# Sixteen gate products between the last two matmuls of a weight chunk instead of behind them

## The reference, cut to what matters

```python
q = (xi @ w_query) ...                       # queries, scores against sub_keys
top_s, top_c = lax.top_k(cand, PEER_TOPK)    # 16 experts per token and head
g = jax.nn.softmax(top_s, axis=-1)
u = jnp.take(expert_down, idx, axis=0)
act = jax.nn.gelu(jnp.einsum('btd,bthkd->bthk', xi, u))
v_sel = jnp.take(expert_up, idx, axis=0)
return jnp.einsum('bthk,bthkd->btd', g * act, v_sel)
```

## Time and profile before

| what | us |
|---|---|
| median of 3 executions | 2059.5 (2059.19 to 2060.71) |
| the profiled execution, whole | 2064.05 |
| its span, from first to last instruction | 2062.2 |
| PE busy, of the span | 2041.3 (99%) |
| DVE busy | 1639.3 (79%) |
| ACT busy | 1356.3 (66%) |

### The profile page before, as it was taken

One profiled execution on the slowest core, in us unless ns is written; L12 is line 12 of the kernel. 1 busy time (PEld: TensorE's weight loads), 2 busy tenths in 40 slices (PEclk: granted clock), 3 DMA queues, 4 the chain that ended last, 5 costly groups with the idle time before them and its releaser, 6 DMA issues.

```text
span 2062.2 us, 31647 instructions
## 1 busy us (share of the span) xinstructions
PE 2041.3 (99%) x11776; PEld 1749.0 (85%) x11776; DVE 1639.3 (79%) x2971; ACT 1356.3 (66%) x2303; POOL 373.5 (18%) x183
## 2 busy tenths in 40 slices
PE   8999999999999999999999999999999999999998
PEld 7788988888888888887888888888888888888888
DVE  7968988889869999877589888899689998743456
ACT  6665688878756666566646888777566666544674
POOL 1448800000000000012378100000000000045341
PEclk9999999999999999999999999999999999999999
DMA  6455855555566566664357655555656555676444
GB/s 231 153 156 168 238 171 169 173 165 167 171 190 203 190 213 202 206 210 143 120 167 222 192 169 168 170 174 167 191 179 208 205 194 188 225 217 197 130 157 139
DMA packets 108461, 376.26 MB, mean 182 GB/s; under 512 B 12372, under 2 KB 17908, under 8 KB 107412
## 3 DMA queue, kind: packets, MB, share of 16 engines
q1 hardware_dynamic: 107444, 369.00, 56.8%
q0 software_dynamic: 864, 5.24, 1.2%
HBM read 367.87 MB, written 1.08 MB: 179 GB/s over the span
## 4 chain that ended last, share of the span: by engine, by line
PE 92%; DVE 5%; ACT 1%; DMA 1%; issue 1%; POOL 0%; SPq 0%; DVEq 0%; ACTq 0%
PE ps L211 29%; PE ps L212 14%; PE ps L205 14%; PE ps L207 14%; PE ps L206 14%; PE ps L1126 3%; DVE WL L192 1%; DMA raw<-in_l_up_dram 1%; PE ps L1105 1%; DVE arena L818 1%; PE ps L1149 1%; DVE arena L815 0%; PE ps L2394 0%; PE ps L2418 0%; PE ps L1152 0%
## 5 line engine op out<-in xcount | busy, mean ns | idle before, releaser
L186 ACT ACTIVATE WH<-raw 128x1024 fp32r<-128x1024 f32 (+1 forms) x680 | 701.7, 1036 | 304.5 <-PE ps L207 186.7
L211 PE MATMUL ps<-X,WH 128*128 128x512 f32 x2528 | 895.9, 398 | 0.1
L212 PE MATMUL ps<-X,WL 128*128 128x256 f32 x2528 | 707.0, 280 | 0.0
L192 DVE TENSOR_TENSOR WL<-raw,WH 128x1024 fp32r<-128x1024 f32 (+1 forms) x554 | 661.9, 1197 | 39.0 <-ACT WH L186 38.2
L198 POOL TENSOR_TENSOR WL<-raw,WH 128x1024 fp32r<-128x1024 f32 x126 | 319.1, 2556 | 1572.6 <-ACT WH L186 1570.5
L211 PEld LDWEIGHTS ps<-X,WH 128*128 128x128 f32 x2528 | 474.0, 188 | 107.8 <-issue 0.6
L212 PEld LDWEIGHTS ps<-X,WL 128*128 128x128 f32 x2528 | 477.2, 189 | 0.1
L205 PE MATMUL ps<-WH,X 128*128 128x512 f32 (+1 forms) x784 | 310.4, 396 | 1.6 <-DVE X L417 0.9
L207 PE MATMUL ps<-WH,X 128*128 128x512 f32 (+1 forms) x784 | 305.4, 390 | 0.0
L206 PE MATMUL ps<-WL,X 128*128 128x512 f32 (+1 forms) x784 | 305.1, 389 | 0.0
L205 PEld LDWEIGHTS ps<-WH,X 128*128 128x128 f32 x784 | 147.5, 188 | 36.9 <-issue 4.5
(11 more groups left out here) (355 smaller groups left out, 2640.2 us busy)
## 6 DMA issues: line engine op xcount, KB each, us to landing
raw<-in_l_down_dram SPq DMA_DIRECT2D x256, 512.0 KB, 3.6
raw<-in_l_up_dram SPq DMA_DIRECT2D x256, 512.0 KB, 4.2
raw<-in_l_wq_dram SPq DMA_DIRECT2D x32, 512.0 KB, 3.5
raw<-in_w_qk_dram SPq DMA_DIRECT2D x24, 512.0 KB, 3.7
raw<-in_w_gates_dram SPq DMA_DIRECT2D x24, 512.0 KB, 3.5
raw<-in_l_nat_dram SPq DMA_DIRECT2D x16, 512.0 KB, 3.5
raw<-in_l_wout_dram SPq DMA_DIRECT2D x16, 512.0 KB, 3.6
raw<-in_l_win_dram SPq DMA_DIRECT2D x16, 512.0 KB, 4.0
```

The lines of the kernel that those rows point to most:

```text
L186: a.activation(WH[:, i % NW, 0:w], raw[:, i % NW, 0:w], ACT.Copy).then_inc(w_high, 1)
L192: v.tensor_tensor(WL[:, i % NW, 0:w], raw[:, i % NW, 0:w], WH[:, i % NW, 0:w], ALU.subtract).then_inc(w_low_v, 1)
L211: t.matmul(PS[:, bank, :], w[0], X2[:, k, :, :].rearrange("p w t -> p (w t)"), start=first, stop=False)
L212: return t.matmul(PS[:, bank, 0:256], w[1], X2[:, k, 0, :], start=False, stop=last)
```

## The change

`two` takes a callable `amid` and calls it between its two matmuls. In the chunks that have a gate block, the loop hands `products` to the eighth step and no longer calls it behind the chunk.

```diff
-        def two(t, bank, w, k, first, last):
+        def two(t, bank, w, k, first, last, amid=None):
 
             t.matmul(PS[:, bank, :], w[0], X2[:, k, :, :].rearrange("p w t -> p (w t)"), start=first, stop=False)
+            if amid:
+                amid()
             return t.matmul(PS[:, bank, 0:256], w[1], X2[:, k, 0, :], start=False, stop=last)
...
                 b = down_bank(c)
+                s, r = divmod(c - SPREAD - 4, PACE)
+                gates = (lambda: products(t, l, s)) if r == 0 and 0 <= s < GROUPS else None
                 for k in range(8):
                     w = [v[:, (down + c) % NW, k * 128:k * 128 + 128] for v in (WH, WL)]
                     if c >= WIDE or c < EARLY:
-                        m = two(t, b, w, k, k == 0, k == 7)
+                        m = two(t, b, w, k, k == 0, k == 7, gates if k == 7 else None)
...
-                s, r = divmod(c - SPREAD - 4, PACE)
-                if r == 0 and 0 <= s < GROUPS:
-                    products(t, l, s)
```

## The result

The changed kernel takes 2063.14 us (median of 22 executions, 2057.11 to 2069.89) where the kernel before, run on the same chip, takes 2059.99 us (22 executions, 2058.77 to 2062.41). The ratio over all executions is 1.0018, 95% interval 1.001 to 1.0026: slower, by 3.15 us between the medians and by 3.6 us between the means (2063.76 and 2060.12). The forecast of no change does not hold, though the difference is smaller than the 4.1 us that the prediction took as the least that can be told, and the time lies in its range.

The account below looks back on a forecast made before the run. TensorE was taken as the bound, 99% busy and waiting for nobody in the changed stage. The terms summed 0 + 0 + 0 + 0 + 0, so the forecast was the median before, 2059.5 us, range 2055.4 to 2065.0.

Parts of the forecast that it names:

- The block's place: Eighth 512 to the next chunk's first 256: 1.58 us before and after the move, 64 x 0.00 = 0.
- second late load: Rival: the 512 behind the split pair also gets its weight load late, +5.1 us at most, 2064.6 us; chance 0.06.
- The first gate load: Block's first weight load: waits behind a 512 too, no gain; if covered, 0.6 to 1.3 us gained, 3.8 at most.
- The waits of the block: What the block waits for is needed 0.12 us earlier; 2.8 us of lead stay in the tightest block: nothing.
- `w_used`: Signal to ACT's queue in chunks with a block comes 0.9 to 1.0 us later, some 6 us left: costs nothing.
- `prod`: Gate block's result, which DVE waits for, comes 0.12 us earlier, off the path: nothing.
- The rhythm after a block: TensorE's periods between blocks, 9.31 or 9.47 us: share of long ones stays, 0; bounds 2.4 us less, 7.5 more.
- slower by the rhythm: Rival: restarting with a 256 behind the block always leads to the long rhythm, +7.5 us, 2067.0 us; chance 0.13.
- Faster by cover and rhythm: Rival: gate load lies under the 512 and no period is long, -3.7 us, 2055.8 (at most -6.2, 2053.3); chance 0.16.

Follow-up runs that it names:

- late `w_used` by itself: Kernel before, blocks in the old place, but in chunks with a block `w_used` is raised by the next chunk's first 512: 2058.9 us, ratio 0.9997.
- early tables: Picked experts turned five matmuls earlier, inside chunk 24, to spare TensorE's wait at chunk 26: 2061.52 us on the kernel before, 2056.66 on the changed kernel.
- one restart more: Kernel with 256, block, 512 in the last step, plus the small products behind chunk 0 parted, half moved into chunk 1: 2055.52 us, ratio 0.9970.
- the 256 ahead of the block: Changed kernel, but in the last step the 256 stands ahead of the gate block and the 512 behind it: 2056.53 us, ratio 0.9987.

## Why the prediction was wrong, point by point

**The block's place: right.** 1.57 us against 1.58 worked out, with every part as listed: the first gate load 0.22 us behind the start of the 512 (285.45), about where the next matmul is due (0.23 to 0.24), 0.90 us of block (285.46 to 286.36), the next 512 at 0.20 of the record (286.56), its 256 0.24 behind. No second late load.

**The first gate load: right, by the row and not by the rule.** The Trainium skill, page "TensorE: Matmul & The Clock Gate", section "Step-by-step: what each phase is for", says that a weight load is pulled ahead of matmuls in flight when the row groups do not conflict or the load goes to the background weight buffer. The trace shows no such lead behind a 512, as behind a 256: PEld stood idle for 0.16 us, and the load started with the gate product, 0.22 us behind the start of the 512. Which buffer the load goes to, no row shows. "When the 256 is over", in the prediction, is a reading of the distances: by the modelled ends of the rows the 256 lasts to 287.24 and the 512 to 285.62, past the start of the gate load.

**The waits of the block, `w_used`, `prod`: right.** No wait of TensorE in the rows after; late `w_used` by itself left the time at 0.9997 of before.

**The rhythm after a block: the step that failed.** The prediction put the bounds at -2.4 and +7.5 us and then chose: "I take that this share stays: 0". The price of a long period was right (0.16 us said; 4.7 us for 31 of them measured, 0.15 each), and so was the list of what can move the time. Wrong was how often. If the three groups of times are taken as no, one and two long layers, the changed kernel had 13 + 2 x 7 = 27 long layers of 44, where the forecast rested on 15 long periods of 62. In the two profiles of the old order with the wait at chunk 26, 2 of 4 layers go in turn; with the three that have early tables it is 7 of 10. At 4.7 us a long layer and 2.4 a layer in turn, the first share gives 2 x 27/44 x 4.7 - 2 x 0.5 x 2.4 = 5.8 - 2.4 = 3.4 us, and the second 5.8 - 3.4 = 2.4 us; measured are 3.6 us between the means. This is an estimate, since few executions have a profile.

Two things in the step led there. It used the 62 restarts with a 512 as evidence on restarts with a 256, the very thing that the change exchanges, and it used them again against the rival "slower by the rhythm" ("47 of 62 restarts did not"). And it counted periods, as if each drew anew. A layer draws once: the rows of before already had one layer all short and one strictly in turn, which is what a state handed from block to block looks like; the prediction itself says that what was there before the block decides, and then does not reckon with it. The outcomes to weigh were whole layers, at 0, 2.4 and 4.7 us each, and an even chance for the unseen restart to leave a layer long would have given 2 x 0.5 x 4.7 - 2.4 = +2.3 us.

**The rivals.** "Slower by the rhythm" was the mechanism, and its form, that a restart with a 256 always leads to the long rhythm, was too strong: that restart made no short rhythm long, and kept a long one unless the block split the longest pair. "Faster by cover and rhythm" is wrong in its cover; its rhythm half, no long period, is what several of the experiments reach.

## What to carry to other kernels

When one engine is the bound and waits for nobody, look at the distances between its starts before and after each disturbance: a repeating stream can have more than one steady rhythm, and an edit that changes with which instruction it restarts can change which one holds, far beyond the place edited. When executions of one kernel stand in groups at equal distances, look for a state that is drawn once and kept, and for the wait that draws it; changing the order of the restart, or taking that wait away, tells more than more executions. And do not carry a share over from the kind of event that the change takes away.

## What the runs showed of the hardware

A stream of 512 and 256 column matmuls on four-byte numbers, at full granted clock with nobody waiting, ran at 353.3 ns a pair (361, 349, 350 in a cycle of three) or at 346.7 ns (all alike, or 350 and 343 in turn), 1.9% apart, and kept either for as long as nothing came between, as over the 151 pairs of the early stretch (long in 26 of 26 layers, and short in the two with one restart more). Small products in between, or a wait of 0.2 us, can move it from one to the other. In the changed order one rule held at all 100 blocks that met the long rhythm, by which of the three pairs the block split: the longest, and the short rhythm followed (4 of 4); another, and it stayed long (96 of 96). Behind a 512 as restart the long rhythm was never kept (116 of 116 in the old order, 5 of 5 with the 256 ahead of the block). What within TensorE makes the cycle, no run here shows.
